# Hybrid gMLP and Conformer decoder layer on eight cores: weight loads issued ahead, norms and a layer norm summed on VectorE, prelude reordered

## The reference, cut to what matters

```python
x = x + 0.5 * swiglu_ffn(rms_norm(x, g1), w_gu1, w_dn1)
h = rms_norm(x, g_mix)
ua, va, glu_a, glu_b, gate_a, gate_b = split(h @ w_in)
u = gelu(ua); v = layer_norm(gelu(va))
s = per chunk of 128 and head: tril(w_s[h]) @ v + b_s;   y_a = (u * s) @ w_pa
g = glu_a * sigmoid(glu_b)                                # with 30 rows of state ahead of it
c = depthwise_conv(g, width 31) + b_dw
y_b = silu(layer_norm(c)) @ w_pb
x = x + (sigmoid(gate_a) * y_a + sigmoid(gate_b) * y_b) @ w_out
x = x + 0.5 * swiglu_ffn(rms_norm(x, g2), w_gu2, w_dn2)
y = rms_norm(x, g_fin)
```

## Time and profile before

| | before |
|---|---|
| time, three runs | 3491.16 us median (3490.33 to 3492.99) |
| profiled execution | 3496.27 us; span of core 2 3494.7 us |
| spans of the cores | 3480.9 to 3494.7 us, granted clock 0.965 to 0.967 |
| TensorE matmul | busy 3253.0 us (93%), 21555 instructions |
| VectorE | busy 856.9 us (25%), 1448 instructions |
| ScalarE | busy 466.4 us (13%), 909 instructions |
| chain that ended last | PE 91%, DMA 5%, DVE 2%, ACT 1%, issue 1% |
| HBM | 468 MB read, 33 MB written |

### The profile page before, as it was taken

How to read it: one execution, slowest core, us unless ns; L and a number is a source line. 1 busy time by engine, 2 the same in 40 slices (tenths; PEclk the granted TensorE clock), 3 DMA queues, 4 the chain that set the end, 5 groups by cost and what they waited for, 6 DMA issues and landing times.

```text
span 3494.7 us, 51300 instructions; the slowest of 8 cores (3480.9 to 3494.7 us)
## 1 busy us (share of the span) xinstructions
PE 3253.0 (93%) x21555; PEld 2067.1 (59%) x21556; DVE 856.9 (25%) x1448; ACT 466.4 (13%) x909; POOL 128.1 (4%) x246
## 2 busy tenths in 40 slices
PE   6999999999999756579899999999999999999997
PEld 2566666666665434347756666666666666666664
DVE  2212122121126221222643111112412112112115
ACT  3000000000003100014721000000300000000002
POOL 0000000000000000000000000000000000000000
PEclk9999999999999878789999999999999999999998
DMA  6436434334345343352344334337333434434434
GB/s 155 74 61 123 80 59 81 69 66 85 66 103 127 67 85 55 78 115 59 65 87 73 71 70 71 71 69 177 58 72 71 84 63 78 73 58 82 73 63 119
DMA packets 74112, 284.30 MB, mean 81 GB/s; under 512 B 9888, under 2 KB 36768, under 8 KB 52000
## 3 DMA queue, kind: packets, MB, share of 16 engines
q0 software_dynamic: 34848, 216.62, 35.6%
q1 hardware_dynamic: 39040, 64.40, 6.3%
HBM read 468.14 MB, written 32.87 MB: 143 GB/s over the span
## 4 chain that ended last, share of the span: by engine, by line
PE 91%; DMA 5%; DVE 2%; ACT 1%; issue 1%; POOL 0%; SPq 0%; DVEq 0%; ACTq 0%; POOLq 0%
PE ps L192 91%; DMA arena<-w_glu 4%; ACT arena L195 1%; DVE arena L205 1%; DMA arena<-xin 1%; ACT L195 0%; DVE arena L209 0%; DVE arena L198 0%; DMA vsamp<-arena 0%; DMA arena<-gd 0%; POOL arena L949 0%; DMA gd<-arena 0%; SPq L949 0%; DVEq L940 0%; DVE arena L201 0%
## 5 line engine op out<-in xcount | busy, mean ns | idle before, releaser
L192 PE MATMUL ps<-arena 128*128 128x364 bf16 (+5 forms) x21555 | 3253.0, 313 | 220.7 <-DMA arena<-w_glu 141.6
L192 PEld LDWEIGHTS ps<-arena 128*128 128x128 bf16 (+1 forms) x21556 | 2067.1, 98 | 1406.5 <-issue 282.4
L198 DVE TENSOR_TENSOR arena<-arena,ps 128x364 bf16<-128x364 f32 (+9 forms) x472 | 237.0, 515 | 1838.9 <-PE ps L192 1836.4
L195 ACT ACTIVATE arena<-ps 128x364 f32<-128x364 f32 (+1 forms) x528 | 241.5, 463 | 2574.4 <-PE ps L192 2524.5
L205 DVE SCALAR_TENSOR_TENSOR arena<-ps,arena 128x364 f32<-128x364 f32 (+5 forms) x451 | 241.1, 539 | 501.2 <-PE ps L192 500.9
L198 DVE TENSOR_TENSOR arena<-arena 128x512 bf16<-128x512 f32 (+7 forms) x168 | 185.3, 1115 | 67.3 <-PE ps L192 44.2
L195 ACT ACTIVATE arena<-arena 128x364 bf16<-128x364 f32 (+6 forms) x276 | 152.8, 631 | 268.5 <-PE ps L192 191.7
L205 DVE SCALAR_TENSOR_TENSOR arena<-arena 128x364 bf16<-128x364 f32 (+4 forms) x196 | 101.2, 594 | 1.8 <-DVE arena L209 0.2
L949 POOL DMA_DIRECT2D arena<-w_gu x88 | 46.6, 529 | 1173.3 <-PE ps L192 1132.8
L949 POOL DMA_DIRECT2D arena<-w_dn x64 | 33.8, 528 | 773.8 <-PE ps L192 761.6
L195 ACT ACTIVATE arena<-ps,arena 128x272 bf16<-128x272 f32 (+3 forms) x76 | 38.0, 500 | 102.9 <-PE ps L192 102.8
(11 more groups left out here) (10 smaller groups left out, 15.9 us busy)
## 6 DMA issues: line engine op xcount, KB each, us to landing
arena<-w_gu POOLq DMA_DIRECT2D x88, 1024.0 KB, 8.1
arena<-w_dn POOLq DMA_DIRECT2D x64, 704.0 KB, 6.2
arena<-w_glu POOLq DMA_DIRECT2D x16, 1024.0 KB, 11.7
arena<-w_gate POOLq DMA_DIRECT2D x16, 1024.0 KB, 8.7
arena<-w_pab POOLq DMA_DIRECT2D x16, 1024.0 KB, 9.8
arena<-w_v POOLq DMA_DIRECT2D x8, 1024.0 KB, 9.6
arena<-w_u POOLq DMA_DIRECT2D x8, 1024.0 KB, 8.1
arena<-w_out POOLq DMA_DIRECT2D x8, 1024.0 KB, 10.3
```

The source lines that it names most:

```text
L192: return P.op("pe", lambda e: e.matmul(out, lhsT, rhs, start=start, stop=stop), deps)
L195: return P.op("act", lambda e: e.activation(out=out, in_=in_, func=func, **kw), deps)
L198: return P.op("dve", lambda e: e.tensor_tensor(out=out, in0=in0, in1=in1, op=op), deps)
```

## The change

1. **Weight stream.** All weight loads stand in one list in order of use (`wseq`). `wissue` puts the next on POOL's queue, `wnext` hands out the oldest, and `wdone` releases a slot and issues the next load at once, at that place in the program.
2. **Norms on VectorE.** For the mix, ffn2 and final norms, `RowNorm` squares each finished row on ScalarE and adds it to a float32 accumulator on VectorE, one row behind. Before the last row the sum is split into a bf16 high and low part; two ones-matmuls sum these and a third the last row's square. `finish` of segment s-1 is called after row m = 10 of segment s. The first norm keeps its 16 ones-matmuls per segment.
3. **Prelude.** The x of segment 1 is loaded right after that of segment 0, w0 to w3 wait for parts of x, the x of segment 2 follows w1. Five small matmuls that nothing reads (`warm`) stand before each ones-matmul of segment 0, and 30 after them. The units with jj = 0 alternate gate and up-matmuls (`paced`). The order of the first nine units and the places of the norms of segments 1 and 2 change.
4. **The convolution's layer norm.** After each convolution ScalarE squares its output, still in the shuffled layout, and VectorE adds output and square to two accumulators (`ln_sum`, one convolution behind). At the end these are folded and split, and 16 matmuls with four selecting matrices of ones (`PHM`) give mean and mean square (`ln_phase`) in place of the 96. Root, row sums, normalisations and SiLU batches follow from the first V tile on, in a new order. The first GELU waits for these sums.

```diff
+        def wissue(after=()):
+            if wseq:
+                src, n = wseq.pop(0)
+                idx, slot, free = wring.get()
+                wahead.append((idx, slot, P.dma("pool", slot[:, 0:n], src, "w%d" % idx, deps=free + list(after))))
+        def wnext():
+            return wahead.pop(0)
+        def wdone(idx, events):
+            wring.release(idx, events)
+            wissue()
...
+        load_tokens(1, [x_ev[(0, 3)]])
+        def warm(n):
+            bi, bk, bfree = banks.get()
+            lm = None
+            for i in range(n):
+                lm = mm(bk[:, 0:128], ONES, ONES, True, True, deps=[e_ones] + (bfree if i == 0 else []))
+            banks.release(bi, [lm])
...
+        class RowNorm:
...
+            def square(self, k, dep):
+                Xs, s = self.a[1], self.a[3]
+                si, sq, sfree = SQR.get()
+                ea = act(sq[:, 0:self.n], Xs[s][:, k, 0:self.n], AF.Square, deps=[dep] + sfree)
+                self.sqs.append((si, sq[:, 0:self.n], ea))
+            def add(self):
+                if not self.sqs:
+                    return
+                (si, sq, ea) = self.sqs.pop(0)
+                if self.ev is None:
+                    self.ev = ts(self.acc, sq, 1.0, 0.0, ALU.mult, ALU.add, deps=[ea])
+                else:
+                    self.ev = tt(self.acc, self.acc, sq, ALU.add, deps=[ea, self.ev])
+                SQR.release(si, [self.ev])
+            def row(self, k, dep):
+                self.add()
+                self.square(k, dep)
+            def split(self):
...
+                e1 = ts(hi[:, 0:n], self.acc, 1.0, 0.0, ALU.mult, ALU.add, deps=[self.ev] + hf)
+                e2 = tt(lo[:, 0:n], self.acc, hi[:, 0:n], ALU.subtract, deps=[e1] + lf)
...
+            def sum_parts(self):
...
+                l1 = mm(bk[:, 0:n], ONES, hi[:, 0:n], True, False, deps=[e1, e_ones] + bfree)
+                l2 = mm(bk[:, 0:n], ONES, lo[:, 0:n], False, False, deps=[e2])
...
+            def finish(self):
+                gidx, Xs, Hout, s, out = self.a
+                si, sq, ea = self.sqs.pop(0)
+                lm = mm(self.bank[1][:, 0:self.n], ONES, sq, False, True, deps=[ea])
+                SQR.release(si, [lm])
+                norm_rows(gidx, Xs, Hout, self.x0, self.n, s, self.bank, lm, out)
...
                     for s in range(3):
                         for (mp, wi, slot, lev) in held:
...
                             for mi in range(2):
-                                ld, ed = down(W, mp * 2 + mi, mi, s, lev)
-                                x_final[(s, mp * 2 + mi)] = ed
-                                if s > 0:
-                                    run_steps(tail_steps[s - 1], 3)
+                                m = mp * 2 + mi
+                                if m == 10 and s == 0:
+                                    for q in range(3):
+                                        norms[q].add()
+                                if m == 15:
+                                    norms[s].add()
+                                    norms[s].split()
+                                ld, ed = down(W, m, mi, s, lev)
+                                x_final[(s, m)] = ed
+                                if m == 15:
+                                    norms[s].sum_parts()
+                                    norms[s].square(m, ed)
+                                else:
+                                    norms[s].row(m, ed)
+                                if s > 0 and m == 10:
+                                    norms[s - 1].finish()
...
+            if what == "w":
+                return [x_ev[((0, 1), (1, 1), (1, 3))[i]]]
+            if what == "w4":
+                return [x_ev[(2, 1)]]
+            if what == "wl" and i == 1:
+                load_tokens(2, [ev])
...
+        warm(30)
+        ffn(SEG_A, H, HID1, X1, h1,
+            {(1, 0): (lambda: run_steps(steps1[1], 99), None),
+             (1, 2): (None, lambda: run_steps(steps1[2], 99))},
+            normm, DN_SEG, x1f, hook1,
+            [(0, 0), (1, 0), (0, 1), (1, 1), (0, 2), (1, 2), (2, 0), (2, 1), (2, 2)])
...
+        def ln_sum(c):
+            si, sq, e_sq, ci, cnp, wv = sql[c]
...
+                ac["m"] = tt(ACM, ACM, cnp[:, 0:2, :], ALU.add, deps=[e_sq, ac["m"]])
+                ac["s"] = tt(ACS, ACS, sq[:, 0:2, :], ALU.add, deps=[ac["s"]])
+            ac["m"] = tt(ACM, ACM, cnp[:, 2:4, :], ALU.add, deps=[ac["m"]])
+            ac["s"] = tt(ACS, ACS, sq[:, 2:4, :], ALU.add, deps=[ac["s"]])
...
         for c in range(SKEW, KC):
-            wi, slot, lev = wload(w_glu[c], 4096)
+            wi, slot, lev = wnext()
             la = None
             for s in range(3):
-                la = glu_unit(c, slot, lev, s, [])
-            wring.release(wi, [la])
+                la = glu_unit(c, slot, lev, s)
+            wdone(wi, [la])
             glu_out(c)
             glu_in()
             for cc in order.get(c, [c - 1]):
                 conv(cc)
+                if cc > 0:
+                    ln_sum(cc - 1)
                 glu_in()
                 if cc + 2 < KC:
                     cw[cc + 2] = conv_weights(cc + 2)
                 if cc + 3 < KC:
                     cg[cc + 3] = conv_cache(cc + 3)
         conv(KC - 1)
+        ln_sum(KC - 2)
+        ln_sum(KC - 1)
...
-        side = [rowsum(q) for q in range(4)]
-        side += [ln_step(s, k) for s in range(3) for k in range(KC)]
-        side_b = [nothing, nothing, ln_root, nothing, nothing]
+        side = [nothing] * 2 + [ln_phase(i) for i in range(4)] + [nothing, ln_root]
+        side += [rowsum(q) for q in range(4)] + [nothing]
         for q in range(4):
-            side_b += [ln_apply(k) for k in range(4 * q, 4 * q + 4)] + [nothing] * 2
+            for k in range(4 * q, 4 * q + 4):
+                side += [ln_apply(k), nothing]
             if q > 0:
-                side_b.append(ln_silu(range(4 * q - 4, 4 * q)))
-        side_b += [nothing] * 4 + [ln_silu(range(12, 16))]
+                side.append(ln_silu(range(4 * q - 4, 4 * q)))
+        side += [nothing] * 3 + [ln_silu(range(12, 16))]
```

More of the change, by code:

```diff
@@ L215, in pvc @@
             return PV[:, g * 16 + k:g * 16 + k + 1]
-        def wload(src, n, after=()):
-            idx, slot, free = wring.get()
-            ev = P.dma("pool", slot[:, 0:n], src, "w%d" % idx, deps=free + list(after))
-            return idx, slot, ev
+        wseq = []
+        for gu, dn in ((w_gu1, w_dn1), (None, None), (w_gu2, w_dn2)):
+            if gu is None:
+                wseq += [(w_glu[c], 4096) for c in range(KC)]
+                wseq += [(w_v[c], 4096) for c in range(8)] + [(w_u[c], 4096) for c in range(8)]
+                for c in range(KC):
+                    wseq += [(w_gate[c], 4096), (w_pab[c], 4096)]
+                wseq += [(w_out[c], 4096) for c in range(8)]
+            else:
+                for gi in range(4):
+                    wseq += [(gu[gi * 11 + jj], 4096) for jj in range(11)]
+                    wseq += [(dn[gi * 8 + mp], 2816) for mp in range(8)]
+        wahead = []
+        def wissue(after=()):
[8 more added lines that the diff above has]
+            wissue()
         def wk(slot):
@@ L282, in run_steps, with ffn, unit @@
                 steps.pop(0)()
-        def ffn(w_gu, w_dn, segs, Hv, HID, Xs, hready, seg_steps, tail_steps, dn_seg, x_final, hook, first_order):
+        def ffn(segs, Hv, HID, Xs, hready, prep, norms, dn_seg, x_final, hook, first_order):
             hid = {}
             hid_free = {0: None, 1: None, 2: None}
-            def unit(slot, lev, jj, s, steps):
+            def unit(slot, lev, jj, s, paced=False, mid=None):
                 x0, n = segs[s]
@@ L355, in ffn @@
                                 x_final[(s, mp * 2 + mi)] = ed
-                    wring.release(wi, [ld])
+                                norms[s].row(mp * 2 + mi, ed)
+                    wdone(wi, [ld])
                 hook("g", gi)
@@ L454, in build_program, with glu_unit @@
         x1_dead = []
-        def glu_unit(c, slot, lev, s, steps):
+        def glu_unit(c, slot, lev, s):
             x0, n = SEG_A[s]
@@ L871, in build_program @@
         h2 = {}
-        steps2 = {s: rms_steps(PV_F2, X2, H2, SEG_B, s, lambda s_, k: x2f[(s_, k)], h2) for s in range(3)}
+        norm2 = [RowNorm(PV_F2, X2, H2, SEG_B, s, h2) for s in range(3)]
         def out_unit(W, mi, m, s, lev):
@@ L886, in build_program @@
         for mp in range(8 - OUT_SEG):
-            wi, slot, lev = wload(w_out[mp], 4096)
+            wi, slot, lev = wnext()
             lm = None
@@ L891, in build_program @@
                     lm = out_unit(wk(slot), mi, mp * 2 + mi, s, lev)
-            wring.release(wi, [lm])
-        held = [(mp,) + wload(w_out[mp], 4096) for mp in range(8 - OUT_SEG, 8)]
+                    norm2[s].row(mp * 2 + mi, x2f[(s, mp * 2 + mi)])
+            wdone(wi, [lm])
+        held = [(mp,) + wnext() for mp in range(8 - OUT_SEG, 8)]
```

(28 more changed lines are left out.)

222 lines of the change are left out of this document (123 added, 99 removed).

## The result

The changed kernel takes 3351.07 and 3351.99 us against 3490.33 to 3492.99 before: 0.960 of the time, 95% interval [0.957, 0.963]. The forecast was 3346 in a range of 3308 to 3384.

A forecast was written before the change was run, and what follows sets the result against it. Bound: TensorE, in the GLU stage waiting for late w_glu loads behind the cache load. −166.9 + 1.3 + 31.0 − 5.8 − 5.0 = −145.4 from 3496.3 gives 3350.9, on the median's scale 3346 us; range 3308 to 3384.

The forecast's parts named there:

- GLU stage: GLU columns: weight loads issued before the cache load remove 11 waits and the slow clock after them; −166.9 us.
- The last shuffle: After the last GLU column: the wait for gd grows from 8.65 to some 10 us; +1.3.
- Norms: Mix, w_out, tail: TensorE stalls for the split behind reciprocal and 16 products; +13.7, +8.0, +9.3, together +31.0 us.
- Rival B: Mix, w_out, tail: no norm stalls, bursts and drains overlap better; −39 in place of +31, 3276 us; chance 0.10.
- V stage: Last convolution to last V group: four SiLU stalls stay, 169.05 us becomes 163.2; −5.8.
- Prelude: Start to end of the ninth unit: up-matmuls fill VectorE-paced gaps, 107 instead of 112 us; −5 (0 to −12).
- Rival C: GLU columns: SP's queue becomes the bound at 24.6 us per column, 4.6 more, ten times; 3392 us; chance 0.13.
- Rival D: POOL's queue at the cache load: weights still come late, the 166.9 us stay; 3513 us; chance 0.03.

The follow-up runs named there:

- the mixed norms: Changed kernel with rows 0 to 9 summed on VectorE, split before row 13, rows 10 to 15 by ones-matmuls one segment later; 3314.11 us.
- The run with pairs: Changed kernel with V-stage row sums before the shared square root and SiLU in eight batches of two instead of four of four; 3316.82 us lowest.
- the run with held loads: Changed kernel with cache loads issued early and three w_glu loads waiting for the third write of gd; 3343.92 us.

## Why the prediction was right, and where it was not

**GLU stage.** The mechanism held in full: waits for w_glu gone, clock 1.00, columns of 20.02 us, loads ahead of the cache loads, additions hidden ahead of the tap weights. The stream alone gives 152 us, more than the change's 140. The step that failed is "In the new order every write has a load just ahead of it. One such column stands in the trace and ran in 20.02 us without a stall, so I add nothing per column". For the columns that is right. But the first three writes come 5 us apart, at the units' ends of the third segment and not 20 us apart, each with a load beside it, and two consumers without slack stand behind them: the third product, which needs the first of two tiles back from cst, and conv(0), which needs gd. I followed gd and never asked what the new load does to cst, a write of 47 KB that nobody had waited for. It cost 8.3 us of wait and 2.3 of slower matmuls around it (the clock was 0.92 in that stretch), which covers the whole miss of 10.2; holding the loads, with the cache loads issued early, gave 10.6 back before the last shuffle, of which 8.2 were left behind it.

**The last shuffle.** +1.3 forecast, −1.3 measured: the wait is 6.84 us, against 8.65. The price was right: in the column shown above the write of gd landed after 9.3 us, near the 9.9 of the earlier trace rows. The place was wrong: in both kernels the last write comes before its load. After the change it is issued at 1409.23, 0.8 us ahead of the load of w_v beside it, and landed after 2.1 us (3.6 before). "In the new order every write has a load just ahead of it" does not hold for the last one.

**Norms.** The walk along VectorE's queue held: stalls forecast at 9 to 11 us at the mix, measured 10.36 and 7.97; 7.4 and 6 at w_out, measured 6.50 and 4.91; 9 to 11 at the tail, measured 10.37 and 8.65. So the first stalls of the mix and the tail lie where they were put, and the other four 0.4 to 1.1 us below. Drain and addition of a row overlap by a little (0.89 us a pair, not 1.06), which fits the shorter second stalls and tail. In all 1.8 + 11.5 + 7.2 + 6.9 = +27.4 against +31.0. Rival B (no stalls, 3276) fell, and the mixed norms show what it would have taken: nearly the same work on VectorE, in another order. (The tail's terms add up to 60.65, not 60.8, which changes nothing.)

**V stage.** −5.9 against −5.8, with four SiLU stalls of 4.10, 4.08, 4.05 and 5.96 us, and two short waits of 0.84 and 0.91 at the first phases where I had 3.2. The stall at the row sums was 3.87, as taken. The run with pairs shows what the forecast left unasked: these stalls, 27 of its us, could go.

**Prelude.** −7.8 against −5, within its 0 to −12; the greater part is the interleaving, 7.5 of 10.6 us over the eight cores.

**Rival C** (SP's queue at 24.6 us a column) fell because the write of cd takes 3.4 us, not 9.9: it is issued at 1260.35, 12 us after the weight load, which landed after 9.9. SP needs 1263.85 + 1.73 − 1249.07 = 16.5 us of a 20 us column. **Rival D** fell at once: no w_glu wait is left.

The −145.4 is met to 1.1 us, but by a term of +10 that I did not have against five of −0.6 to −2.8 that I had too dear. That these cancel is luck; that no single one but conv(0) is off by more than 2.8 us is not. On the median's scale the forecast was 3346 and the result is 5.5 us above it, because the profiled execution before stood 5.1 above its median and the one after only 0.5.

## What to carry to other kernels

When two steps move past each other, follow every transfer that now runs beside a large load, down to the small writes nobody waited for: what frees a small tile can stand at the head of an in-order engine with the critical work behind it. A burst (a reciprocal and 16 products) that nothing needs soon must stand behind the short step that the other engine waits for; work removed from TensorE is worth nothing if TensorE then waits for its replacement. And cut the batches of a side engine to what the buffers between it and the bounding engine can cover, even at the price of more table loads. An edit that moves one transfer moves its neighbours on the queue too: read the issue times of all of them before you say what the run tests.

## What the runs showed of the hardware

- A write of gd (280 KB) or of cst (47 KB) with no weight load beside it lands in 1.9 to 2.1 us. Issued 0.8 us after a 1 MB load on POOL's queue, with another load following 4.5 us later, the same write of gd took 8.2 us on core 5 and 13.1 on core 0, and that of cst, 0.4 us behind it, 8.0 and 20.3. In the run with held loads a write of cst issued 1.2 us after a load still took 19.7 us (nobody waited). The Trainium skill, DMA: Bandwidth & Descriptors, "Queues, rings and completion order", says that a DMA engine takes turns between its queues packet by packet; by even turns, as an estimate from that rule, the 2 us would have become about 4. The times here are 4 to 11 times those without a load, so a small write pays far more than an even share; why is not shown.
- Which of the two a core gets differs by execution: cores 0, 3, 4 and 7 ended late in the profiled one, cores 1, 3, 5 and 7 in the next. The first write of gd lands just before the third load is issued on the early ones (at 1127.0 against 1128.6 on core 5) and after it on the late ones (1135.4 against 1132.1 on core 0), and the next writes move with it; what decides it stays open.
- The small matmuls that nothing reads, put in while x arrives, did not make the ninth unit end earlier: 100.7 to 104.8 us with them, 100.6 to 102.2 without.
